# Summing selected expert rows for two prompt tiles: row gathers against dense products over the whole V table

## The reference

```python
q = (xb @ w_query).reshape(tn, PEER_HEADS, 2, PK_HALF)             # 8 heads, 2 halves of 128
s = jnp.einsum('thkd,hknd->thkn', q, sub_keys)
top_s, top_i = lax.top_k(s, PK_TOPK)                               # 16 of 128 keys, per half
...                                                                # 256 sums of pairs, top 16 again
experts = jnp.take_along_axis(cand_i, best_j, axis=-1)             # 8 x 16 = 128 of 16384 experts per token
gates = jax.nn.softmax(best_s, axis=-1)
act = jax.nn.gelu(jnp.einsum('thkd,td->thk', expert_u[experts], xb), approximate=False)
out = jnp.einsum('thk,thkd->td', gates * act, expert_v[experts])
x = layer_norm(DEEPNORM_ALPHA * x + out, ln2_g, ln2_b)
```

## Time and profile before

| | |
|---|---|
| Three runs, median (lowest to highest) | 5266.74 us (5266.41 to 5269.16) |
| Span of the profiled execution | 5258.6 us |
| Busy: TensorE, VectorE, ScalarE, GpSimd | 76%, 63%, 18%, 28% of the span |
| Moved by the DMA engines | 1462 MB, 278 GB/s over the span |
| Of it by GpSimd's queue (gathers, picks, stores) | 996 MB, 46.9% of the 16 engines' span |
| `peer`: dense U beside gathers / sum of tiles 1 to 3 | to 4172 us / 4235 to 5258.6 us |

### The profile page before, as it was taken

One profiled execution on the slowest core, in us unless ns is written; L12 is line 12 of the kernel. 1 busy time (PEld: TensorE's weight loads), 2 busy tenths in 40 slices (PEclk: granted clock), 3 DMA queues, 4 the chain that ended last, 5 costly groups with the idle time before them and its releaser, 6 DMA issues. The chain is left out here.

```text
span 5258.6 us, 61057 instructions
## 1 busy us (share of the span) xinstructions
PE 3984.0 (76%) x24165; PEld 3204.5 (61%) x24165; DVE 3327.4 (63%) x4454; ACT 933.3 (18%) x1274; POOL 1476.5 (28%) x1641
## 2 busy tenths in 40 slices
PE   8999999999968887999998999999999700000000
PEld 7999999999955666997896555555555400000000
DVE  2323333343336666334445977879788799999998
ACT  2222232232222233223341000000000000000000
POOL 0000000000044441000010222222222377777774
PEclk9999999999978888999999999999999855555555
DMA  4332332333269996326566999999999999999998
GB/s 158 115 129 96 104 111 96 109 101 104 80 235 353 346 356 248 110 102 219 165 222 222 418 421 418 396 418 421 421 420 421 394 403 410 409 410 410 409 410 330
DMA packets 339992, 1462.12 MB, mean 278 GB/s; under 512 B 87268, under 2 KB 116356, under 8 KB 199928
## 3 DMA queue, kind: packets, MB, share of 16 engines
q0 software_dynamic: 175328, 995.65, 46.9%
q1 hardware_dynamic: 133608, 430.42, 22.9%
q10 hardware_dynamic: 30768, 32.11, 1.8%
HBM read 1362.71 MB, written 94.75 MB: 277 GB/s over the span
## 5 line engine op out<-in xcount | busy, mean ns | idle before, releaser
L2242 DVE SCALAR_TENSOR_TENSOR i_acc<-i_row,i_cf,i_acc 128x2048 f32<-128x2048 f32 x571 | 1344.8, 2355 | 156.7 <-DMA i_row<-in_expert_v,i_ei 120.4
L2049 PE MATMUL i_p_h<-i_xT,i_ut 128*128 128x384 f32 x4096 | 1322.0, 486 | 0.0
L2049 PEld LDWEIGHTS i_p_h<-i_xT,i_ut 128*128 128x128 f32 x4096 | 778.8, 190 | 540.8 <-DMA i_xT<-tmp_x1T 0.3
L2358 POOL DMA_INDIRECT i_row<-in_expert_v,i_ei x576 | 545.9, 948 | 635.5 <-DVE i_acc L2242 511.2
L265 PE MATMUL a_acc<-a_xh,a_wh 128*128 128x288 f32 x3104 | 672.4, 298 | 18.5 <-DVE a_xl L491 13.4
L265 PE MATMUL a_acc<-a_xh,a_wl 128*128 128x288 f32 x3104 | 665.6, 296 | 0.0
L265 PE MATMUL a_acc<-a_xl,a_wh 128*128 128x288 f32 x3104 | 665.0, 296 | 0.0
L265 PEld LDWEIGHTS a_acc<-a_xh,a_wh 128*128 128x128 f32 x3104 | 499.7, 189 | 30.0 <-issue 27.8
L2233 DVE CUSTOM_DVE_ANT_0 i_row<-i_row,i_acc 128x2048 f32<-128x2048 f32 x192 | 433.7, 2286 | 126.0 <-DMA i_row<-in_expert_u,i_ei 124.1
L265 PEld LDWEIGHTS a_acc<-a_xl,a_wh 128*128 128x128 f32 x3104 | 500.8, 189 | 0.0
L265 PEld LDWEIGHTS a_acc<-a_xh,a_wl 128*128 128x128 f32 x3104 | 500.8, 189 | 0.0
(11 more groups left out here) (314 smaller groups left out, 5337.8 us busy)
## 6 DMA issues: line engine op xcount, KB each, us to landing
i_ut<-in_u_tiles SPq DMA_DIRECT2D x128, 1024.0 KB, 9.6
a_w<-in_w_in SPq DMA_DIRECT2D x97, 1024.0 KB, 4.9
f_w<-in_w_out SPq DMA_DIRECT2D x32, 1024.0 KB, 5.1
f_w<-in_w_query SPq DMA_DIRECT2D x32, 1024.0 KB, 5.2
tmp_Ha<-i_ho ACTq DMA_DIRECT2D x128, 192.0 KB, 9.2
tmp_uT<-a_out POOLq DMA_DIRECT2D x65, 288.0 KB, 2.4
f_w<-in_w_bs SPq DMA_DIRECT2D x16, 1024.0 KB, 4.8
tmp_xcT<-f_cv POOLq DMA_DIRECT2D x32, 288.0 KB, 4.3
```

The lines of the kernel that those rows point to most:

```text
L2049: last = nc.tensor.matmul(p_h[:, e % 2, 0:ND], ut[:, e % RU, k * P:(k + 1) * P], xT[:, k, :], start=(k == 0), stop=(k == KT - 1))
L2242: v.scalar_tensor_tensor(acc, row[:, m % R, :], cf[:, j, k:k + 1], acc, ALU.mult, ALU.add).then_inc(row_used, 1)
L2358: pool.indirect_dma_start(row[:, m % R, :], None, table, bass.IndirectOffsetOnAxis(index, axis=0)).then_inc(row_in[m % R], 16)
```

## The change

Tiles 1 and 2 (`DENSE`) no longer gather V. TensorE multiplies the whole V table with a table of coefficients, expert by token, that is zero where a token didn't pick the expert. Tile 3 (`LATE`) gathers as before.

- The DRAM table `Wd` (16384 x 256 floats) holds the gates. It is zero-filled in the first stage by SyncE, 16 transfers of 1 MB from a broadcast row. In `peer` GpSimd adds the gates into it with 256 indirect transfers (`scatter`), each with one gate for each of 128 tokens, spread between the gathers m = 168 to 375. Before every 16th it waits until all earlier ones have landed.
- SyncE waits for all scatters before it issues u tile 122 of 128, loads the first gate tiles (`gate_tiles`: 256 experts of `Ha` and of `Wd`), and then the last six u tiles and the first V tiles.
- The new loop `e` = 0 to 127: SyncE loads 128 rows of V (`load_v`, ring of four in `ut`), ScalarE casts them (`v_hi`), VectorE makes the low part (`v_lo`). For each pair of tiles ScalarE takes the Gelu of the `Ha` block (`gate_gelu`), VectorE multiplies with the gates (`gate_mul`), and the product is split as well (`gate_hi`, `gate_lo`). TensorE (`dense_v`) adds three products into eight PSUM banks, four for each token tile.
- Beside it tile 3 gathers: 9 rows for 8 tiles, from tile 6 on; its sum `sum3` now lies in SBUF, since the banks are in use. The norms of tiles 0 and 4 are hooked into the loop, those of 1 and 2 come behind it.
- GpSimd issues all gathers of tile 4 before the picks. The U table is laid out in another order of experts by the host, `Ha` accordingly. Routing buffers share memory with new ones.

```diff
@@ project_and_prompt, SyncE: behind each of 16 loads
+                    sp.dma_start(gate_rows[(tau - 1) * P:tau * P, :], io["zeros"].to_broadcast([P, D])).then_inc(zeroed, 16)
@@ peer
+    DENSE = (1, 2)
+    LATE = 3
+    NV = 2 * P
+    RV = 4
+    NG = NK * NK // (2 * P)
+        sums = {0: acc, 4: acc, 3: sum3[:, :], 1: ps[:, 0:4, :].rearrange("p a n -> p (a n)"), 2: acc}
+        adds_by = lambda e: 0 if e < 6 else min(PICKS, (e - 5) * 9 // 8)
@@ SyncE
+                def gate_tiles(n):
+                    if n >= 2:
+                        sp.wait_ge(gl_out, n - 1)
+                    sp.dma_start(hb[:, n % 2, :, :], dr["Ha"][n, :, :, 0:NV]).then_inc(hw_in[n % 2], 16)
+                    sp.dma_start(wb[:, n % 2, :, :], dr["Wd"][n]).then_inc(hw_in[n % 2], 16)
+
+                def load_v(e):
+                    if e < RV:
+                        sp.wait_ge(e_done, NE + (-6, -5, -2, -1)[e] + 1 + 4)
+                    else:
+                        sp.wait_ge(vl_out, e - RV + 1)
+                    sp.dma_start(ut[:, (e + 2) % RV, :], v_rows[e // 2, e % 2]).then_inc(v_in[e % RV], 16)
...
                     for e in range(max(8 * lo, RU), 8 * hi):
+                        if e == NE - 6:
+                            sp.wait_ge(routed, 5)
+                            sp.wait_ge(added, 16 * 2 * PICKS)
+                            for m in range(4):
+                                sp.wait_ge(h_stored[m], 16)
+                            gate_tiles(0)
+                            gate_tiles(1)
                         sp.wait_ge(e_done, e - RU + 1 + 4)
...
+                for e in range(4, NE):
+                    load_v(e)
+                    if e % 2 == 1 and e // 2 + 1 < NG:
+                        gate_tiles(e // 2 + 1)
@@ TensorE
+                def dense_v(e):
+                    n, r = e // 2, e % 2
...
+                    if r == 0:
+                        pe.wait_ge(gl_out, n + 1)
+                    pe.wait_ge(vl_out, e + 1)
+                    for i in range(2):
...
+                        cols = slice(i * P, i * P + P)
+                        for t, (g, v) in enumerate(((gh, vh), (gh, vl), (gl, vh))):
+                            for c in range(4):
+                                last = nc.tensor.matmul(ps[:, 4 * i + c, :], g[:, n % 2, r, cols], v[:, e % 2, 512 * c:512 * c + 512],
+                                                        start=(e == 0 and t == 0), stop=(e == NE - 1 and t == 2))
@@ ScalarE
+                def gate_gelu(n):
+                    act.wait_ge(hw_in[n % 2], 32 * (n // 2) + 32)
+                    nc.scalar.activation(hb[:, n % 2, :, :], hb[:, n % 2, :, :], ACT.Gelu).then_inc(act_g, 1)
...
+                def v_hi(e):
+                    act.wait_ge(v_in[e % RV], 16 * (e // RV) + 16)
+                    if e >= 2:
+                        act.wait_ge(v_done, e - 1)
+                    nc.scalar.copy(vh[:, e % 2, :], ut[:, (e + 2) % RV, :]).then_inc(vh_out, 1)
...
+                gate_hi(0)
+                act.wait_ge(e_done, NE + 4)
+                for m in range(4):
+                    act.wait_ge(h_stored[m], 16 * (NE // 4))
+                v_hi(0)
+                for e in range(NE):
+                    n = e // 2
+                    if e + 1 < NE:
+                        v_hi(e + 1)
+                    if e % 2 == 0 and n + 1 < NG:
+                        gate_hi(n + 1)
+                    if e % 2 == 1 and n + 2 < NG:
+                        gate_gelu(n + 2)
@@ VectorE
+                def gate_mul(n):
+                    dve.wait_ge(act_g, n + 1)
+                    v.tensor_tensor(hb[:, n % 2, :, :], hb[:, n % 2, :, :], wb[:, n % 2, :, :], ALU.mult).then_inc(mul_out, 1)
...
+                def v_lo(e):
+                    dve.wait_ge(vh_out, e + 1)
+                    v.tensor_tensor(vl[:, e % 2, :], ut[:, (e + 2) % RV, :], vh[:, e % 2, :], ALU.subtract).then_inc(vl_out, 1)
...
+                for e in range(NE):
+                    n = e // 2
+                    if e + 1 < NE:
+                        v_lo(e + 1)
+                    if e % 2 == 0 and n + 1 < NG:
+                        gate_lo(n + 1)
+                    if e % 2 == 1 and n + 2 < NG:
+                        gate_mul(n + 2)
+                    for k in range(adds_by(e - 1), adds_by(e)):
+                        if k % UN == 0:
+                            coefs(LATE, k, k + UN, 3 + k // UN)
+                        add(LATE, k)
...
+                for j in DENSE:
                     finish(j)
+                for j in DENSE:
+                    variance(j)
+                for j in DENSE:
+                    for part in range(3):
+                        norm(j, part)
@@ GpSimd
+                def scatter(s):
+                    j, k = DENSE[s // PICKS], s % PICKS
+                    if k == 0:
+                        pool.wait_ge(gates_out, place[j] + 1)
+                    if k % TOPK == 0 and s > 0:
+                        pool.wait_ge(added, 16 * s)
+                    pool.indirect_dma_start(w_flat, bass.IndirectOffsetOnAxis(hx[:, j, k:k + 1], axis=0), gt[:, j, k:k + 1], None,
+                                            compute_op=ALU.add).then_inc(added, 16)
+
+                def scatters_by(m):
+                    return 0 if m < 168 else PICKS * (m - 167) // 88 if m < 256 else min(2 * PICKS, PICKS + PICKS * (m - 255) // 120)
...
+                for k in range(PICKS):
+                    if k + UN < PICKS:
+                        pick(k + UN)
+                    if k >= R:
+                        gather(first_v[LATE] + k, io["expert_v"], ei[:, LATE, k:k + 1])
```

More of the change, by code:

```diff
@@ L1955, in peer @@
         row_used = tl.sem("i_row_used")
+        added = tl.pool_sem("i_added")
         pick_in = [tl.pool_sem(f"i_pick_in{k}") for k in range(2)]
@@ L1961, in peer @@
         hi_in = tl.sem("i_hi_in")
+        joined = tl.sem("i_joined")
+        hw_in = [tl.sem(f"i_hw_in{k}") for k in range(2)]
+        act_g = tl.sem("i_act_g")
+        mul_out = tl.sem("i_mul_out")
+        gh_out = tl.sem("i_gh_out")
+        gl_out = tl.sem("i_gl_out")
+        v_in = [tl.sem(f"i_v_in{k}") for k in range(RV)]
+        vh_out = tl.sem("i_vh_out")
+        vl_out = tl.sem("i_vl_out")
+        v_done = tl.sem("i_v_done")
+        tile_done = tl.sem("i_tile_done")
+        x1_last = tl.sem("i_x1_last")
+        mean_out = tl.sem("i_mean_out")
         squares = tl.sem("i_squares")
@@ new lines, in norm @@
+                def norm(j, part):
+                    n, p = rows_of(j), done[j]
+                    rr = rest[j][0:n, :]
+                    if part == 0:
+                        dve.wait_ge(root_out, p + 1)
+                        dve.wait_ge(gb_in, 32)
+                        v.reciprocal(st[0:n, j, 9:10], st[0:n, j, 8:9])
+                        dve.drain()
+                        v.tensor_scalar(rr, rr, st[0:n, j, 1:2], st[0:n, j, 9:10], ALU.add, ALU.mult)
+                    if part == 1:
+                        v.tensor_tensor(rr, rr, gb[0:n, 0, :], ALU.mult)
+                    if part == 2:
+                        v.tensor_tensor(rr, rr, gb[0:n, 1, :], ALU.add)
+                    dve.drain()
+                    if part == 2:
+                        dve.sem_inc(normed, 1)
@@ L2351, in _ @@
-                variance(3)
-                norm(3)
+                v_lo(0)
+                gate_lo(0)
+                for e in range(NE):
+                    n = e // 2
[9 more added lines that the diff above has]
+                        add(LATE, k)
+                    if e == 2:
+                        variance(0)
+                    if e in (4, 5, 6):
+                        norm(0, e - 4)
+                    if e == 3:
+                        join_halves()
+                    if e == 8:
+                        variance(4)
+                    if e in (10, 11, 12):
+                        norm(4, e - 10)
+                    if e == 120:
+                        finish(LATE)
+                    if e == 122:
+                        variance(LATE)
+                    if e in (124, 125, 126):
+                        norm(LATE, e - 124)
@@ L2375, in _ @@
                     gather(P + k, io["expert_u"], ei[:, 4, k:k + 1])
+                    scatters(P + k)
                 for k in range(PICKS):
                     gather(first_v[0] + k, io["expert_v"], ei[:, 0, k:k + 1])
-                for k in range(HP - R):
+                    scatters(first_v[0] + k)
+                for k in range(HP):
                     gather(first_v[4] + k, io["expert_v"], ei[:, 4, k:k + 1])
+                    scatters(first_v[4] + k)
                 pool.wait_ge(routed, 5)
```

277 lines of the change are left out of this document (146 added, 131 removed).

## The result

The changed kernel takes 5237.66 us, the median of four runs (5226.32 to 5239.73), and the kernel before 5266.57 us beside it on the same chip. The ratio is 0.9936, with a 95% interval of 0.9922 to 0.9950: 0.64% faster, where 1.5% was forecast. The profiled run took 5226.32 us and has a span of 5224.6, against 5258.6 before. So the two profiles differ by 34.0 us; the forecast had 78.6.

The account below looks back on a forecast made before the run. From 4235 to 5238 VectorE and the transfers bind nearly equally. V begins at 4356, plus 794 loop and 30 end: 5180 us span, plus 8.1 to the median: 5188; range 5080 to 5385, likeliest case 5120 to 5256.

Parts of the forecast that it names:

- What bounds before: Sum over gathered V rows, 4235 to 5238: VectorE and the transfers bind nearly equally, 2.61 us a row.
- The loop: Loop over 128 V tiles: VectorE and transfers each need 6.08 us a tile, 6.3 taken, 794 us in all.
- Add into SBUF: Tile 3's adds in the V loop: moving the sum from PSUM to SBUF leaves them about 2.3 us each.
- GpSimd held in the loop: Picks and gathers in the V loop, behind VectorE operations reading two SBUF tiles: 2.06 to 2.76 us each.
- A scatter on GpSimd: Between gathers 168 and 375: each scatter costs GpSimd 1.25 us, like a pick; 16 with 11 gathers take 33.7 us.
- The wait ahead of each 16th: GpSimd's wait for landed scatters: 11 us each in gathers 168 to 255, about 15 in 256 to 334.
- Gathers 256 to 335: Second stretch with scatters: 15 gathers and 16 scatters take 38.6 of 53 us, the wait just fits; +10 us.
- SyncE's wait: Before u tile 122: TensorE stops at 4110, last scatter lands at 4265, TensorE begins with V at 4356.
- the dear scatter: Rival before V: a scatter takes 1.6 us of GpSimd, the wait 17; V begins at 4552, total 5384; chance 0.22.
- The hidden case: Rival: scatters cost no time, V begins at 4270, loop takes 769 us, total 5078; chance 0.15.
- the lock: Rival in the V loop: GpSimd and its lock with VectorE bind, 6.9 us a tile, total 5256; chance 0.10.
- the SBUF sum at half rate: Rival in the V loop: an add takes 4.7 us, a tile 8.7, total 5460; last two rivals together 0.03.
- that rival: V loop: TensorE waits for split operands, falls to its lower clock, 10.7 us a tile; last two rivals together 0.03.

Follow-up runs that it names:

- the bursts: Changed kernel with SyncE's scatter wait behind the last u tile, and each 16 scatters over 8 gathers (later 11), the next three without: 5192.06 us, 0.9694 of the kernel before.

## Why the prediction was right or wrong

The direction was right, and so was the loop; what comes ahead of V was taken too short, by the GpSimd time of a scatter above all. The 44.6 us between 34.0 and 78.6 are these: V began at 4406.5 and not at 4356 (+50.5), loop -4.8, end -1.1.

- **What bounds before**: right for the place. On another chip the gathers took 31 us longer at lower GB/s with VectorE's busy time the same, so there the transfers bound them.
- **The loop**: 789.2 us from V tile 0 to the start of the last product against 794, period 6.22 against 6.3. Of the two sums of 6.08 us the transfers' fits (6.09 at 409 GB/s), and VectorE was busy 266 of 300 us, 89%, where over 90% was forecast. TensorE's 24 matmuls are 5.63 us, 0.234 each, not 0.223, which stayed under the period.
- **Add into SBUF**: 2.35 us, as taken. "Vector Engine (DVE) Microarchitecture Reference", section 7, of the Trainium skill, would have made it half as fast; the trace disagrees, 2346 ns against 2355 with PSUM.
- **GpSimd held in the loop**: picks took 2.00 us, near the 2.06 of the earlier trace rows, and didn't bind, as the run without picks shows.
- **A scatter on GpSimd: the step that failed.** It was taken as a pick's 1.25 us from start to start, "above, I know no limit" with it; 1.88 was measured. Sixteen of them and eleven gathers are 44 us of GpSimd and not 33.7, beyond the 39.3 of the gathers' own pace, so that GpSimd became the limit before any waiting. Gathers 168 to 256 took 405 us in place of 314, 91 more, where some 40 were forecast and 17 for the transfers of the scatters in the half where these are full. GpSimd is busy or waits for landings throughout (a window, then its waits in it):

```profile
3470.70:3875.50 404.80, 403.64 (x1274) 239.15 (x1273) 270.63 (x336) 23.36 (x44) 295.18 (x216) 1.00 1.01 365
```

```profile
POOL tmp_Wd L2540 <- DMA tmp_Wd<-i_gt,i_hx: 46.0, 7, 24.3
POOL tmp_Wd L2540 <- issue: 36.9, 121, 0.3
POOL i_row L2527 <- issue: 22.9, 75, 0.3
```

  Busy and between two issues it spends 355 us, where the forecast had 270, and waits 46 us for landings, where it had 88. The runs bear this out: with plain writes the stretch takes 52 us less in either kernel (353 for 405, 324 for 376), with the waits hidden 29 less. The 10 that are left when both are done are no price of the transfers: in that run GpSimd still waits 17.5 us for landings, and TensorE's delay in the kernels with plain writes freed some transfers.
- **The wait ahead of each 16th**: 11, then 15 us forecast. Measured 24 us once, then 1.5 to 9 and next to nothing for the last three, 68 us in all. The mechanism was right and the size too large; it gave back part of the error of the term above.
- **Transfers of a scatter**: 0.13 us taken, at most 0.11 by the bursts.
- **Gathers 256 to 335**: +9 us against +10, besides the 17 for transfers. **335 to 375**: 132 us against 128, and that is luck: the 3.2 us a gather were 38.6 us of GpSimd and 10 of waiting for 15 gathers, and measured were 49 of GpSimd (16 x 1.88 + 15 x 1.25) and 1.1 us of waiting in the whole stretch.
- **SyncE's wait**: the hole, its place and its cause are right (4129.7 to 4326.9; it begins later than 4110 by the 3.4 us of the stage and by a wait of TensorE for ScalarE of 12.9 us, to no effect). The last scatter landed at 4302 and not at 4265 (+37, of which 3.4 are that later start), and from there to the u tile 24.6 us went by and not 15 (+9.6): the sum had 2.1 MB beside gathers, and not the five more u tiles and the eight rows issued at the same moment. From u tile 122 to V it was 79.6 against 76. The wait's place by itself costs 45 us, which the prediction had not priced apart.
- **Median and span**: the 8.1 us between them were kept for the changed kernel. Its profiled run has 1.7 between its time and its span. With as little in the kernel before, its profiled execution was some 6 us faster than the median, and faster than the fastest of the four runs (5265.5). By the runs' medians the gain is 29 us and not 34.
- **The rivals**: the dear scatter had the right cause, a scatter that holds GpSimd for longer than a pick, and was off in both of its terms: its 1.6 us stood for the time from start to start, which was 1.88, and its wait was 17 us, from which all of its delay in the first half came. The prediction bound the two in one case, though nothing in the trace tied them together. The hidden case falls by the 100 us that gather 335 is late, the lock by the period of 6.22 and by the run without picks, the SBUF sum at half rate by 2346 ns. TensorE kept a granted clock of 0.98 in the loop, so it took the sum over; that rival's 5690 left out 14 tiles at the lower clock.

## What to carry to other kernels

Price a DMA that is issued from an engine's queue on that engine first, and price a form that the trace doesn't show (here: one that adds) apart from its wait, since the two need not go together. A wait on a load queue goes behind the last load that doesn't need it, and a wait for a landing behind some work that fills it: two edits of order, without any change of what is computed, took 102 us off here and made a change of 0.6 to 1.2% one of 3.1%. Where a whole time is to be compared between chips, count from a common point and name the part that differs.

## What the runs showed of the hardware beyond what was expected

- An indirect DMA that adds into DRAM, 128 elements, holds GpSimd for 1.58 us, one that writes 0.98, one that fetches 0.95, with 0.3 us more to the next. The last adding one had landed 1.7 us behind its end on GpSimd.
- The DMA share stayed at 1.01 and 1.02 while the GB/s fell from 420 and 421 to 368 and 377: it was no measure of what the transfers could still take.
- With fetches or plain writes of single elements between the gathers TensorE fell behind: 36 matmuls in 100 us at a granted clock of 0.50 in one run, single matmuls with pauses of up to 2.7 us in another, and no wait for a u tile in either. With adding ones at the same places it didn't. The cause is open.
- Gathers of 8 KB rows ran at 395 and 379 GB/s on one chip and at 410 and 401 on another, the same kernel and part; the kernel that also reads whole tiles had 409 on two chips.
